# Three nested loops of two turns for an expert's further blocks, and block counts carried in registers

## The reference

```python
    experts = grp[:, None] * EXPERTS_PER_GROUP + top_i.astype(jnp.int32)   # [256, 2]
    weights = p_grp * top_p / jnp.sum(top_p, axis=-1, keepdims=True)
...
    def run_block(args):
        tok, e = args
        xb = xf[tok]                                   # the tokens of this block
        hid = jax.nn.silu(xb @ w_gate[e]) * (xb @ w_up[e])
        return hid @ w_down[e]                         # 1024 -> 512 -> 1024
...
    y = jnp.zeros((n_tok, d), f32).at[buf_t].add(outs.reshape(cap, d) * buf_w[:, None])
```

## Time and profile before

| | |
|---|---|
| median of 3 runs | 1007.04 us (1006.73 to 1007.93) |
| the profiled execution | 1006.75 us, of which the span from the first to the last instruction is 1004.6 us |
| busy: TensorE / VectorE / ScalarE / GpSimd | 807.6 / 490.3 / 357.7 / 51.9 us |
| weights of the experts | 28 x 3 loads of 2 MB |
| chain that ended last, by engine | PE 58%, DMA 21%, DVE 10%, issue 5%, ACT 5% |

### The profile page before, as it was taken

The page is one execution under the profiler, slowest core; times in us unless marked ns, Lnnn a source line. Parts: engine busy times, 40 slices in busy tenths (PEclk is TensorE's granted clock), DMA queues, the critical chain, the costliest instruction groups (busy, mean ns, idle before and its releaser), DMA issues.

```text
span 1004.6 us, 21163 instructions
## 1 busy us (share of the span) xinstructions
PE 807.6 (80%) x8049; PEld 656.3 (65%) x8050; DVE 490.3 (49%) x787; ACT 357.7 (36%) x490; POOL 51.9 (5%) x145
## 2 busy tenths in 40 slices
PE   5999879799999998879999697686665665767463
PEld 5999669699999998868989664343332332334231
DVE  3544687758787854665797532242212211232222
ACT  5432486355554644353884231111101101110102
POOL 4000100000000000101040000000000000000000
PEclk8999899899999999998999798998877878898877
DMA  7586222259898755352337846999999999999993
GB/s 265 173 281 246 96 79 90 84 209 343 293 312 307 254 191 185 95 168 86 126 91 294 341 182 252 366 426 424 429 427 424 428 427 427 424 429 427 423 430 147
DMA packets 89007, 278.72 MB, mean 277 GB/s; under 512 B 8031, under 2 KB 67850, under 8 KB 71562
## 3 DMA queue, kind: packets, MB, share of 16 engines
q1 hardware_dynamic: 88270, 276.86, 71.5%
q10 hardware_dynamic: 700, 1.36, 0.4%
HBM read 277.15 MB, written 1.05 MB: 277 GB/s over the span
## 4 chain that ended last, share of the span: by engine, by line
PE 58%; DMA 21%; DVE 10%; issue 5%; ACT 5%; PEld 1%; SPq 0%; PEldq 0%; ACTq 0%; DVEq 0%
DMA Whi<-in_w_up 20%; PE bank L1832 10%; PE bank L381 9%; PE bank L383 9%; PE bank L382 9%; PE bank L1853 3%; DVE Whi_r L321 2%; PE acc L432 1%; PE bank L1548 1%; PE bank L1551 1%; PE acc L1548 1%; PE acc L1553 1%; PE bank L1553 1%; PE acc L1551 1%; PE bank L1844 1%
## 5 line engine op out<-in xcount | busy, mean ns | idle before, releaser
L381 PE MATMUL bank<-R_r,Whi_r 128*128 128x256 f32 x800 | 233.9, 292 | 18.0 <-DVE R_r L2112 7.3
L382 PE MATMUL bank<-R_r,Whi_r 128*128 128x256 f32 x800 | 230.9, 289 | 0.0
L383 PE MATMUL bank<-R_r,Whi_r 128*128 128x256 f32 x720 | 207.0, 287 | 0.0
L381 PEld LDWEIGHTS bank<-R_r,Whi_r 128*128 128x128 f32 x800 | 157.9, 197 | 23.2 <-issue 18.3
L382 PEld LDWEIGHTS bank<-R_r,Whi_r 128*128 128x128 f32 x800 | 158.2, 198 | 0.1
L383 PEld LDWEIGHTS bank<-R_r,Whi_r 128*128 128x128 f32 x720 | 141.4, 196 | 0.0
L2603 DVE TENSOR_TENSOR V<-V,bank 64x256 f32<-64x256 f32 x34 | 14.4, 424 | 239.7 <-ACT V L1315 239.7
L1832 PE MATMUL bank<-Whi,S 128*32 128x256 f32 x832 | 63.1, 470 | 46.9 <-DMA Whi<-in_w_up 34.0
L1315 ACT ACTIVATE V<-bank 64x256 f32<-64x256 f32 x34 | 12.8, 376 | 212.0 <-PE bank L1832 212.0
L312 ACT ACTIVATE Whi_r<-Wlo 128x1024 fp32r<-128x1024 f32 x64 | 64.0, 1050 | 66.8 <-PE bank L383 65.9
L2057 DVE TENSOR_TENSOR Whi_r<-Wlo,Whi_r 128x2048 fp32r<-128x2048 f32 x33 | 75.6, 2290 | 25.0 <-ACT Whi_r L1108 12.2
(11 more groups left out here) (493 smaller groups left out, 1579.5 us busy)
## 6 DMA issues: line engine op xcount, KB each, us to landing
Wlo<-in_w_in SPq DMA_DIRECT2D x24, 1024.0 KB, 5.2
Wlo<-in_w_gate_up SPq DMA_DIRECT2D x22, 1024.0 KB, 5.1
Whi<-in_w_gate SPq DMA_DIRECT2D x10, 2048.0 KB, 25.6
Whi<-in_w_up SPq DMA_DIRECT2D x10, 2048.0 KB, 30.1
Whi<-in_w_down SPq DMA_DIRECT2D x10, 2048.0 KB, 31.8
Wlo<-in_w_gate SPq DMA_DIRECT2D x9, 2048.0 KB, 27.7
projR<-in_w_up SPq DMA_DIRECT2D x9, 2048.0 KB, 38.0
Wlo<-in_w_up SPq DMA_DIRECT2D x9, 2048.0 KB, 32.2
```

Source lines behind the costliest of these rows:

```text
L381: pe.matmul(o, w_hi[:, c], tile(x_hi, k), start=(k == 0), stop=False)
L382: pe.matmul(o, w_hi[:, c], tile(x_lo, k), start=False, stop=False)
L383: mm = pe.matmul(o, w_lo[:, c], tile(x_hi, k), start=False, stop=(k == KT - 1))
```

## The change

GpSimd, ScalarE, TensorE and VectorE get their further blocks from a common function, `further_windows`: three nested loops of two turns, with steps 4, 2 and 1, in which the block is w = a + b + c. Each level has an `If` ahead of its body, which asks whether the expert has any block left in that part.

On ScalarE, TensorE and VectorE the block count of the next expert and the sum of the blocks so far are kept in two registers (`expert_registers`). They are set once ahead of the loop; within each expert's first block `load_next` reads the next expert's count into the first register and adds this expert's to the second. At the head of an expert `snap` takes both as they are. TensorE takes the total at the end from the register as well. SyncE and GpSimd keep their `value_load`s.

```diff
+        def further_windows(e, windows, window):
+            with e.If(windows > 1):
+                with e.Fori(0, NWIN, 4) as a:
+                    with e.If(windows > a + 1):
+                        with e.Fori(0, 4, 2) as b:
+                            with e.If(windows > a + b + 1):
+                                with e.Fori(1, 3) as c:
+                                    with e.If(windows > a + b + c):
+                                        window(nc.s_assert_within(
+                                            a + b + c, 1, NWIN - 1,
+                                            skip_runtime_bounds_check_because="w < windows <= NWIN"))
+
+        def expert_registers(e):
+            now, seen = e.alloc_register("windows_now"), e.alloc_register("windows_seen")
+            e.reg_load(now, tbl[0:1, NW_AT:NW_AT + 1])
+            e.reg_mov(seen, 0)
+            return now, seen
+
+        def load_next(e, now, seen, i, par, windows):
+            e.reg_load(now, tbl[0:1, bass.ds(i * NBUF + (NW_AT + par + 1), 1)])
+            e.reg_add(seen, seen, windows)
...
+            pe_now, pe_seen = expert_registers(pe)
+
             def expert(i, par):
                 gate, up, down = Wx[par]
-                windows = pe.value_load(tbl[0:1, bass.ds(i * NBUF + (NW_AT + par), 1)],
-                                        min_val=0, max_val=NWIN)
+                windows = pe.snap(pe_now, min_val=0, max_val=NWIN)
                 with pe.If(windows > 0):
-                    before = pe.value_load(tbl[0:1, bass.ds(i * NBUF + (WB_AT + par), 1)],
-                                           min_val=0, max_val=MAXWIN)
+                    before = pe.snap(pe_seen, min_val=0, max_val=MAXWIN)
...
                         combine().then_inc(sem("comb"), 1)
+                        if w is None:
+                            load_next(pe, pe_now, pe_seen, i, par, windows)
 
                         pe.wait_ge(*upto("slot_rows_out", 2))
                         pe.wait_ge(*upto("hid", now))
...
                     window(None, before + 1)
-                    with pe.If(windows > 1):
-                        with pe.Fori(1, NWIN) as w:
-                            with pe.If(windows > w):
-                                window(w, before + w + 1)
+                    further_windows(pe, windows, lambda w: window(w, before + w + 1))
...
-            total = pe.value_load(tbl[0:1, NV5 * NO:NV5 * NO + 1], min_val=1, max_val=MAXWIN)
+            total = pe.snap(pe_seen, min_val=1, max_val=MAXWIN)
```

More of the change, by code:

```diff
@@ L917, in expert @@
                     gather(0, True)
[L918 to L921, removed]
+                    further_windows(pool, windows, gather)
                     if par < NBUF - 1:
@@ L1304, in _, with window @@
             act.wait_ge(*upto("tbl_ready"))
+            act_now, act_seen = expert_registers(act)
             def expert(i, par):
-                windows = act.value_load(tbl[0:1, bass.ds(i * NBUF + (NW_AT + par), 1)],
-                                         min_val=0, max_val=NWIN)
+                windows = act.snap(act_now, min_val=0, max_val=NWIN)
                 with act.If(windows > 0):
-                    before = act.value_load(tbl[0:1, bass.ds(i * NBUF + (WB_AT + par), 1)],
-                                            min_val=0, max_val=MAXWIN)
-                    def window(now):
+                    before = act.snap(act_seen, min_val=0, max_val=MAXWIN)
+                    def window(now, first=False):
                         act.wait_ge(*upto("gu_done", now))
@@ L1316, in window @@
                                        ).then_inc(sem("sil"), 1)
+                        if first:
+                            load_next(act, act_now, act_seen, i, par, windows)
                         act.wait_ge(*upto("ht_done", now))
@@ L1323, in window @@
                         act.activation(yp_hi, yb, ACT.Copy).then_inc(sem("yp_hi"), 1)
[L1325 to L1329, removed]
+                    window(before + 1, True)
+                    further_windows(act, windows, lambda w: window(before + w + 1))
                     if par < NBUF - 1:
@@ L2592, in _, with window @@
             dve.wait_ge(*upto("slot_rows_out", 2))
+            dve_now, dve_seen = expert_registers(dve)
             def expert(i, par):
-                windows = dve.value_load(tbl[0:1, bass.ds(i * NBUF + (NW_AT + par), 1)],
-                                         min_val=0, max_val=NWIN)
+                windows = dve.snap(dve_now, min_val=0, max_val=NWIN)
                 with dve.If(windows > 0):
-                    before = dve.value_load(tbl[0:1, bass.ds(i * NBUF + (WB_AT + par), 1)],
-                                            min_val=0, max_val=MAXWIN)
-                    def window(w, now):
+                    before = dve.snap(dve_seen, min_val=0, max_val=MAXWIN)
+                    def window(w, now, first=False):
                         dve.wait_ge(*upto("sil", now))
@@ L2619, in window @@
                                                  op1=ALU.add).then_inc(sem("oh"), 1)
+                        if first:
+                            load_next(dve, dve_now, dve_seen, i, par, windows)
                         dve.wait_ge(*upto("wt_now", now))
@@ L2628, in window @@
                                           ).then_inc(sem("yp_lo"), 1)
[L2630 to L2634, removed]
+                    window(0, before + 1, True)
+                    further_windows(dve, windows, lambda w: window(w, before + w + 1))
                     if par < NBUF - 1:
```

## The result

The changed kernel took 1001.15 us (median of 4 runs, 999.66 to 1001.69), against 1007.14 (4 runs, 1006.73 to 1007.93) for the kernel before on the same chip: 6.0 us less by the medians. The ratio on record is 0.9936, 95% interval 0.9924 to 0.9949, which is 5.1 to 7.7 us. The prediction was 1001.5. The profiled execution of the changed kernel took 999.66 us, with a span of 997.9; by the prediction it would have been 1001.2.

The account below looks back on a forecast made before the run. TensorE was taken to bound the kernel up to expert 4's weight-load issue, DMA from there to the last landing. Start 5.0 + end 1.1 - last group 0.6 = 5.5 us saved: median 1001.5 us, range 1000.2 to 1004.2.

Parts of the forecast that it names:

- What bounds the kernel: Expert stage: TensorE sets the pace to about 631 us, then DMA until the last landing near 983 us.
- Parts 1 and 2: TensorE's hole ahead of expert 1: nested loops save 1.59 us, register counts 1.37; 4.59 becomes 1.63.
- Part 3: Next expert's count loaded in the first block, some 0.5 us per expert on three engines: hidden, taken as 0.
- Part 4: Entering the nested loops: 0.92 us more sequencer work, charged at 0.25 us, twice ahead of expert 4's issue.
- Part 5: Expert 1's 64 gate/up matmuls: with the shorter hole the clock stays up, 3.70 us for 6.23, saving 2.53.
- The start in sum: Expert 4's weight loads issued 5.0 us earlier, and the last landing earlier by as much.
- The end: Behind the last landing: 1.1 us saved without value loads, 0.6 charged for a last gate/up group of mean length.
- part 1: Leaving the nested loops behind expert 0: 1.59 us saved, or an estimated 0.8 at about 108 ns a branch.
- Rival (b): Mid-block loads and nest entry cost their bounds, code fetch at expert 1 about 0.5 us: 1003.3 us; chance 0.10.
- rival (c): Longer loop outgrows an engine's instruction memory, fetched anew every pass: 1009.5 us at 1.6 us a place; chance 0.03.
- DMA pauses behind expert 4: Sign against the prediction: weight traffic stopping after expert 4's loads would make it fall; no size given.

Follow-up runs that it names:

- the delay at the second expert: Changed kernel plus four value loads with dropped results on TensorE at the head of experts 1, 4, 7 and on: 1004.24 us.
- filler at the end: Changed kernel plus matmuls nobody reads (two and four) in TensorE's waits for weights, in experts 24 to 27 alone: 997.39 us.
- filler from the seventh expert on: Changed kernel plus matmuls nobody reads (three and four) in TensorE's waits for weights, in every expert from the seventh: 1006.67 us.

## Why the prediction was right

**What bounds the kernel.** Right. Only what came ahead of expert 4's issue or behind the last landing counted: TensorE's part alone gave all the gain of the start, the others' part only the 0.94 at the end (and 0.4 outside the span), and the stop of 5.6 us plus 2.8 of a cold group behind that issue nothing that shows.

**Parts 1 and 2, the hole.** Forecast 1.63 us, measured 1.32. Leaving the nest took 2.23 us (608.62 to 610.85) for the 2.47 put down, since an addition and its neighbour are one instruction; the head of the next expert took 0.54. The rows by line of TensorE's sequencer, 608.4 to 611.4, changed kernel:

```profile
L554 PEldq COMPARE_BRANCH  x2: 76/142/207, 610.0 to 610.7; - x2
L554 PEldq FUSED_REGOPS  x1: 47/47/47, 610.2 to 610.2; - x1
...
L556 PEldq COMPARE_BRANCH  x2: 76/146/216, 609.0 to 609.7; - x2
...
L558 PEldq COMPARE_BRANCH  x1: 73/73/73, 608.7 to 608.7; - x1
```

Five back edges instead of six and two refused `If`s instead of five. The prices taken from the earlier trace rows held: 0.21 taken, 0.08 falling through.

**Part 3, the loads in mid-block.** Free, as forecast. In expert 0 the load on TensorE lies between 591.65 and 592.21 us, and the wait for `hid` behind it is over at 592.64:

```profile
L572 PEldq TENSOR_LOAD <-tbl x1: 323/323/323, 591.8 to 591.8; - x1
...
L1864 PEldq EVENT_SEMAPHORE  x1: 51/51/51, 592.6 to 592.6; - x1
```

**Part 4, entering the nest.** Charged at 0.25 us twice; it came nearly free. The way from the block's end to the wait for `xw` grew from 0.44 to 1.08 us, 0.64 more for the 0.92 put down (fused additions again), and that stays within the sequencer's head start of 1.45: expert 0's second block follows with no hole, and only expert 1's pays 0.12 (3.62 for 3.50). The step named the cover rightly and had the price too high.

**Part 5, the clock.** 2.53 forecast and found, and this is where the chance was right rather than the proof: at 2.68 us of hole the clock fell, at 2.06 it stayed, and elsewhere in these traces it did the opposite at like lengths (last section).

**The start in sum.** 5.0 forecast, 5.67 measured (3.27 + 2.53 - 0.12); 5.55 of it reached the last gate/up start.

**The end.** Table load 1.13 us behind the activation, forecast 1.0. The last group was charged at its mean, 5.76; this profile drew 6.26 of a range of 4.97 to 6.59, others here 5.0 to 6.55. A draw, not a step. The mean was read a little high: the trace of before has 15 gate/up groups behind a wait for weights from 717 us on, 5.66 us on average, so the charge should have been 0.5. (A side sum was off too: with 0.108 us for a branch, part 1 comes to about 0.9 us saved, not 0.8.)

**What of the number was luck.** The profiled execution was put at 1001.2 and took 999.66. Of the 1.5 us between, 1.3 is the earlier start of the stage and 0.4 lies outside the span, neither of them in the sum; the counted stretch gave 0.55 more than forecast, the last group took 0.5 more and the end gave 0.1 less. The median came within 0.4 us of the forecast because the other three runs were 1.0 to 2.0 us longer than the profiled one. What is borne out is the terms, not the 0.4.

**Where it fell short.** Rival (b) had the right mechanism, code that has to be fetched, at the wrong place and price: 0.5 us at expert 1, where the stop cost 5.95 at expert 3. Had it come 20 us earlier, the delay at the second expert shows what it would have taken: the whole gain at the start. That no refused `If` showed such a stop in the kernel before was no evidence, since new code lies elsewhere. The 1009.5 of rival (c), code fetched anew on every pass, did not come: the instruction queue has 26 transfers for 25. And "DMA pauses behind expert 4" and a hole at a later place weren't watched for together; they should have been: a hole is harmless only where the loads queued ahead of it outlast it.

## What to carry to other kernels

In a loop that is fed by transfers, find the issue that opens the unbroken traffic and the last landing; price only what lies ahead of the one or behind the other, engine by engine, and leave the rest alone. For TensorE a hole in issue has two prices, its own length and the clock behind it, so two savings that are each half of what is needed can be worth more together. Fill a wait to keep the clock only where the group behind it ends on the critical path (here the last four experts, 2.5 us by the profile), and count the filler against the longest stretch of work, not the usual one.

## What the runs showed of the hardware

- **A taken branch can take 6 us.** 5.80 to 6.44 us in six kernels on TensorE, beside an instruction transfer under weight traffic at a DMA share of 1.03; 0.45 with the loop's head moved, 1.14 and 1.58 in the kernels with filler. It ends 1.4 to 1.5 us behind the end of that transfer in all eight where it took over 1 us.
- **The length of a hole alone doesn't tell whether the clock falls.** At the head of expert 1 it stayed behind 1.32, 1.35, 1.74 and 2.06 us without a matmul and fell behind 2.68, 3.12 and 3.99. But elsewhere in the stage it stayed behind 2.57 (after, group at 676.23) and 2.96 (filler at the end, 891.12) and fell behind 2.56 (filler from the seventh expert on, 630.06) and 2.65 (filler at the end, 629.54); the earlier trace rows has a fall behind 2.0.
- **Taking the loads away did not change how far the sequencer runs ahead** of the down matmuls: leaving the nest begins at 608.62, 1.46 us before the matmuls end at 610.08, where it was 1.45.
